# A three-layer block on one Trainium2 core: the first layer's columns from unscaled tiles, its head norms in two groups, its heads and pooling interleaved with columns

## The reference, cut to what matters

```python
h = rms_norm(x, norm_mix[0])
z = h @ w_in                                   # 1024 x 2048
u, q, k, v = jnp.split(z, [512, 1024, 1536], axis=-1)
p = multiscale_pool_minus_identity(u)          # windows 2, 4, 8, 16, one per 128 columns
p = einsum('bsgc,gcd->bsgd', p, pool_w) * pool_scale
a = moba_attention(q, k, v, q_gain, k_gain)    # 8 heads of 64
x = x + concatenate([p, a]) @ w_out

# inside moba_attention, with one block of 256 keys:
qn = q * rsqrt(mean(q * q) + eps) * q_gain     # per head and row; kn the same way
logits = qn @ kn.T * 64 ** -0.5 - slope[head] * distance, causal
out = softmax(logits) @ v
```

## Time and profile before

| what | value |
|---|---|
| median of 3 runs | 1214.41 us |
| the profiled execution's own time | 1214.9 us |
| its span in the profile | 1213.1 us |
| granted TensorE clock, mean | 0.96 of full speed |
| busy: PE / DVE / ACT / POOL | 1109.4 / 869.8 / 646.0 / 44.1 us |
| first matmul | 14.01 us |
| first long run of `pa_w_out` matmuls | 138.16 us |
| mean DMA rate | 165 GB/s |

### The profile page before, as it was taken

One profiled execution on the slowest core, in us unless ns is written; L12 is line 12 of the kernel. 1 busy time (PEld: TensorE's weight loads), 2 busy tenths in 40 slices (PEclk: granted clock), 3 DMA queues, 4 the chain that ended last, 5 costly groups with the idle time before them and its releaser, 6 DMA issues.

```text
span 1213.1 us, 20990 instructions
## 1 busy us (share of the span) xinstructions
PE 1109.4 (91%) x8548; PEld 1050.2 (87%) x8548; DVE 869.8 (72%) x1494; ACT 646.0 (53%) x1109; POOL 44.1 (4%) x50
## 2 busy tenths in 40 slices
PE   4769799999998988899999989899999989999996
PEld 3756499999997868789999988789989979999996
DVE  5666599888788448787877776998884577655543
ACT  6334467666554595566556568312224447876431
POOL 0000010000000200100000000000000002000010
PEclk9879899999998988899999989999999989999999
DMA  8422756655555556356666554122332354656541
GB/s 288 123 70 88 242 184 191 194 181 161 191 166 202 206 200 222 96 185 241 243 237 223 175 175 144 44 88 87 104 136 105 122 200 156 192 177 204 177 156 36
DMA packets 60576, 200.41 MB, mean 165 GB/s; under 512 B 6720, under 2 KB 12480, under 8 KB 60352
## 3 DMA queue, kind: packets, MB, share of 16 engines
q1 hardware_dynamic: 59040, 194.85, 48.7%
q10 hardware_dynamic: 1440, 4.22, 1.0%
HBM read 197.99 MB, written 1.05 MB: 164 GB/s over the span
## 4 chain that ended last, share of the span: by engine, by line
PE 71%; DVE 17%; ACT 8%; DMA 2%; issue 2%; SPq 0%; ACTq 0%; DVEq 0%
PE ps L451 71%; DVE wlo L1527 4%; ACT whi L1003 2%; ACT L1003 1%; DVE rst L1556 1%; DVE rq L1736 1%; DVE raw L1533 1%; DMA ring<-rg_w_in 1%; DVE raw L1527 1%; DVE hl L1527 1%; DVE xr L1533 1%; DMA ring<-pa_w_in 1%; ACT rr L1003 0%; ACT L L1003 0%; ACT raw L1003 0%
## 5 line engine op out<-in xcount | busy, mean ns | idle before, releaser
L451 PE MATMUL ps<-hh,whi 128*128 128x256 f32 (+1 forms) x1656 | 489.8, 296 | 56.2 <-DVE wlo L1527 42.7
L451 PE MATMUL ps<-hh,wlo 128*128 128x256 f32 (+1 forms) x1656 | 478.5, 289 | 0.0
L451 PE MATMUL ps<-hl,whi 128*128 128x256 f32 (+1 forms) x1656 | 476.7, 288 | 0.0
L1527 DVE TENSOR_TENSOR wlo<-ring,whi 128x1024 fp32r<-128x1024 f32 (+1 forms) x313 | 375.5, 1214 | 71.9 <-ACT whi L1003 71.0
L451 PEld LDWEIGHTS ps<-hh,whi 128*128 128x128 f32 x1656 | 324.2, 196 | 76.8 <-issue 31.5
L1003 ACT ACTIVATE whi<-ring 128x1024 fp32r<-128x1024 f32 (+1 forms) x313 | 322.6, 1039 | 96.7 <-PE ps L451 63.6
L451 PEld LDWEIGHTS ps<-hl,whi 128*128 128x128 f32 x1656 | 325.3, 196 | 1.5 <-issue 1.0
L451 PEld LDWEIGHTS ps<-hh,wlo 128*128 128x128 f32 x1656 | 324.4, 196 | 0.0
L451 PE MATMUL ps<-hidh,whi 128*128 128x256 f32 x608 | 172.3, 283 | 1.6 <-DVE wlo L1527 1.6
L451 PE MATMUL ps<-hidh,wlo 128*128 128x256 f32 x608 | 172.1, 283 | 0.0
L451 PE MATMUL ps<-hidl,whi 128*128 128x256 f32 x608 | 172.1, 283 | 0.0
(11 more groups left out here) (345 smaller groups left out, 1378.3 us busy)
## 6 DMA issues: line engine op xcount, KB each, us to landing
ring<-ffn_w_in SPq DMA_DIRECT2D x88, 512.0 KB, 4.2
ring<-ffn_w SPq DMA_DIRECT2D x64, 512.0 KB, 4.2
ring<-w_in SPq DMA_DIRECT2D x51, 512.0 KB, 3.6
ring<-ada_w SPq DMA_DIRECT2D x48, 512.0 KB, 4.9
ring<-ffn_w_out SPq DMA_DIRECT2D x32, 448.0 KB, 4.3
ring<-rg_w_in SPq DMA_DIRECT2D x20, 512.0 KB, 4.5
ring<-pa_w_in SPq DMA_DIRECT2D x16, 512.0 KB, 5.9
ring<-ffn_w_out SPq DMA_DIRECT2D x16, 512.0 KB, 3.6
```

The lines of the kernel that those rows point to most:

```text
L451: return e.matmul(o, l, r, start=start, stop=stop)
L1527: return e.tensor_tensor(o, a, b, op)
```

## The change

- All 16 columns of `pa_w_in` are taken from the tiles without the row's scale; `h_tiles(0)`, `early(0)` and the three `lift` go. u is multiplied by `rst` as it leaves PSUM, v by `tk` (the same scale with rows in partitions) as its transposition leaves PSUM, and for q and k the scale cancels in the head norm, where epsilon is multiplied by the row's mean square (`tk[:, 2]`).
- The head norms are done in two groups of four columns, with rows in partitions (`sums`): 8 matmuls with 2 output columns each give a 128x16 tile of means, so the root and the reciprocal work on 16 elements. For q the result is a scalar per partition in `scores`. For k ACT spreads it over 128x256 (`ivk`), PE turns it (`spread`), and DVE multiplies the column by it.
- `scores` starts from slope times distance, made ahead on POOL (`dms`, eight of 128x384, in space of `cosT` and `sinT`), and takes two instructions instead of one.
- One list, `ATTN`, sets the order on PE, ACT and DVE: a number is a column, N is `sums`, B `spread`, S `scores`, P the end of the softmax, T `turn_p`, V the transposition of v, O `values_of` (now two heads at once), G `pool_out`, A `mod_step`. Columns are in the order 4, 8, 5, 9, 6, 10, 7, 11, 12 to 15, 3, 2, 1, 0.
- The pooling's running sums move from DVE to POOL (`pooled`). `pah` and `pal` are made straight from PSUM. `L`, `PT` and `sm` have eight buffers.
- At the start the 32 vectors that the gains need are a DMA of their own, on ACT's queue, x comes in two DMAs instead of eight, and a dummy root loads ACT's table early. The sigmoid moves behind the first head norm.

```diff
+ATTN = [
+    4, 8, 5, 9, 6, ("N", 0), 10, ("B", 0), 7, ("S", 0), 11, ("S", 1), ("P", 0), 12, ("N", 1), ("S", 2), ("P", 1), ("T", 0),
+    13, ("B", 1), ("S", 3), ("P", 2), ("T", 1), ("A",), 14, ("S", 4), ("P", 3), ("T", 2), 15, ("S", 5), ("P", 4), ("T", 3), ("A",),
+    3, ("V",), ("S", 6), ("P", 5), ("T", 4), 2, ("O", 0), ("S", 7), ("P", 6), ("T", 5), ("A",), 1, ("O", 1), ("P", 7), ("T", 6),
+    ("A",), 0, ("T", 7), ("O", 2), ("G", 3), ("A",), ("G", 2), ("A",), ("O", 3), ("G", 1), ("A",), ("G", 0),
+]
...
-                early(0)
-                for i in range(3):
-                    give(("pa_w_in", 4 + i), at_dve, ("lift", i))
-                for ms in ([7, 8], [9], [10], [11], [12], [13], [14], [15]):
-                    project("pa_w_in", ms, 0)
-                    for i in HEAD_NORMS[ms[-1]]:
-                        head_norm(i)
...
+                    linear("pa_w_in", [c], pair(hh[:, :, 0:T], hl[:, :, 0:T]), 8, lambda k: hlow.wait_ge(e, (0, k)))
+                    if c < 4:
+                        give(("pa_w_in", c), at_dve, ("u", c))
+                    elif c < 12:
+                        give(("pa_w_in", c), at_act, ("qk", c - 4))
+                    else:
+                        give(("pa_w_in", c), at_act, ("v", c - 12))
+                    if c == 8:
+                        row_stats()
...
+                    mm(p[:, 0:T], ones, sqa[:, :], True, False)
+                    mm(p[:, 0:T], ones, sqt[:, 2, :], False)
+                    for z in range(2):
+                        zs = slice(z * 128, z * 128 + 128)
+                        mm(p[:, T + 2 * z:T + 2 * z + 2], sqa[:, zs], ones[:, 0:2], True, False)
+                        t = mm(p[:, T + 2 * z:T + 2 * z + 2], sqt[:, 2, zs], ones[:, 0:2], False)
+                    t.then_inc(*stat.up(0))
+                    give(("stat", 0), at_dve, "var")
...
+                def sums(g):
+                    p = take(("n", g))
+                    for j in range(2):
+                        for c in (4, 8):
+                            c += 2 * g + j
+                            a = qk_tile(c)[2]
+                            at_act.wait_ge(e, ("sq", c))
+                            for z in range(2):
+                                t = mm(p[:, z * 8 + 2 * a:z * 8 + 2 * a + 2], sq[:, a, z * 128:z * 128 + 128], blk[:, 0:128:64])
+                    t.then_inc(*at_pe.up(("n", g)))
+                    give(("n", g), at_dve, ("hm", g))
...
+                def spread(g):
+                    p = take(("b", g))
+                    at_act.wait_ge(e, ("ivk", g))
+                    for j in range(2):
+                        for z in range(2):
+                            t = mm(p[:, j * T + z * 128:j * T + z * 128 + 128], ivk[:, z, j, :], ident)
+                    t.then_inc(*at_pe.up(("b", g)))
+                    give(("b", g), at_dve, ("k", 2 * g + 1))
...
+                def column(c):
+                    feed(tail("pa_w_in", c))
+                    if 3 < c < 12:
+                        g, a = qk_tile(c)[1:]
+                        if g:
+                            at_pe.wait_ge(e, ("n", 0))
+                        act(sq[:, a, :], out_of("pa_w_in", c), ACT.Square).then_inc(*at_act.up(("sq", c)))
+                        at_dve.wait_ge(e, "gq")
+                        act(qk[:, c - 4, :], out_of("pa_w_in", c), ACT.Copy, gq[:, :] if c < 8 else P("k_gain")).then_inc(*at_act.up(("qk", c - 4)))
+                    elif c > 11:
+                        act(vf[:, c - 12, :], out_of("pa_w_in", c), ACT.Copy).then_inc(*at_act.up(("v", c - 12)))
+                    if c == 8:
+                        stats(0)
+                        at_dve.wait_ge(e, "var")
+                        act(tk[:, 1, :], tk[:, 0, :], ACT.Sqrt).then_inc(*at_act.up("root"))
...
+                def sums(g):
+                    at_dve.wait_ge(e, ("hm", g))
+                    act(iv[:, g, :], iv[:, g, :], ACT.Sqrt).then_inc(*at_act.up(("hr", g)))
+                    if g == 0:
+                        act(cpar[15], P("c", 0, 8), ACT.Sigmoid).then_inc(*ada_act.up("sig"))
+
+                def spread(g):
+                    at_dve.wait_ge(e, ("iv", g))
+                    if g:
+                        at_pe.wait_ge(e, ("b", 0))
+                    for z in range(2):
+                        i = iv[:, g, z * 8:z * 8 + 8].rearrange("p (j s) -> p j s", j=2)[:, :, 2:4].unsqueeze(3).to_broadcast([128, 2, 2, 64])
+                        t = act(ivk[:, z, :, :].rearrange("p j (s d) -> p j s d", s=2), i, ACT.Copy)
+                    t.then_inc(*at_act.up(("ivk", g)))
...
+                    act(pah[:, g, :], ps[where["po", g]][:, 0:T], ACT.Copy, P("pool_scale", g)).then_inc(*at_act.up(("pah", g)))
...
+                    act(pah[:, 4 + j, :], ps[where["o", j]][:, 0:T], ACT.Copy).then_inc(*at_act.up(("pah", 4 + j)))
...
+            e.dma_start(vec[:, 0:32], d["vec"][:, 0:32]).then_inc(*gains_in.up("all", 16))
             e.dma_start(cst[:, 0:384], d["cst"][:, 0:384]).then_inc(*ones_in.up("all", 16))
-            vecs_in.wait_ge(e, "all")
+            e.dma_start(vec[:, 32:], d["vec"][:, 32:]).then_inc(*vecs_in.up("all", 16))
+            at_dve.wait_ge(e, "dummy")
+            act(dmy[:, :], dmy[:, :], ACT.Sqrt).then_inc(*at_act.up("dummy"))
+            gains_in.wait_ge(e, "all")
             for m in range(8):
-                xin[m].wait_ge(e, m)
+                xin[m // 4].wait_ge(e, m // 4)
                 high_of_h(0, m)
-            feed(-4)
+                if m == 3:
+                    feed(-4)
...
-                    r = rq[:, i % 2, :]
-                    at_pe.wait_ge(e, ("hn", i))
-                    if i > 1:
-                        at_dve.wait_ge(e, ("qk", i - 2))
-                    ts(r, ps[where["hn", i]][:, 0:T], 1.0 / 64, 1e-6, MUL, ADD).then_inc(*at_dve.up(("hm", i)))
-                    at_act.wait_ge(e, ("hr", i))
-                    e.reciprocal(r, r).then_inc(*at_dve.up(("hi", i)))
...
-                    stt(qk[:, i, :], p, gq[:, :] if i < 4 else P("k_gain"), r, MUL, MUL).then_inc(*at_dve.up(("qk", i)))
...
+                def column(c):
+                    feed(tail("pa_w_in", c))
+                    if c < 4:
+                        mean.wait_ge(e, ("rst", 0))
+                        tt(u[:, c, 16:], out_of("pa_w_in", c), rst[:, :], MUL).then_inc(*at_dve.up(("u", c)))
...
+                def sums(g):
+                    at_pe.wait_ge(e, ("n", g))
+                    at_dve.wait_ge(e, "eps")
+                    for z in range(2):
+                        t = ts(iv[:, g, z * 8:z * 8 + 8], ps[where["n", g]][:, z * 8:z * 8 + 8], 1.0 / 64, tk[:, 2, 2 * z:2 * z + 1], MUL, ADD)
+                    t.then_inc(*at_dve.up(("hm", g)))
+                    at_act.wait_ge(e, ("hr", g))
+                    e.reciprocal(iv[:, g, :], iv[:, g, :]).then_inc(*at_dve.up(("iv", g)))
...
+                def spread(g):
+                    at_pe.wait_ge(e, ("b", g))
+                    for v in range(2):
+                        j = 2 * g + v
+                        at_act.wait_ge(e, ("qk", 4 + j))
+                        tt(qk[:, 4 + j, :], ps[where["b", g]][:, v * T:v * T + T], qk[:, 4 + j, :], MUL).then_inc(*at_dve.up(("k", j)))
...
+                    at_pool.wait_ge(e, ("dm", hd))
+                    at_dve.wait_ge(e, ("iv", g))
+                    at_pe.wait_ge(e, ("s", hd))
+                    stt(L[:, hd, 0:128], p[:, 0:128], iv[:, g, a:a + 1], dms[hd][:, 0:128], MUL, ADD)
+                    stt(L[:, hd, 128:384], p[:, 128:384], iv[:, g, 8 + a:9 + a], dms[hd][:, 128:384], MUL, ADD).then_inc(*at_dve.up(("L", hd)))
...
+            def pooled(g):
+                cur = u[:, g, :]
+                at_dve.wait_ge(e, ("u", g))
+                for w in range(g + 1):
+                    s = 1 << w
+                    nxt = (ta, tb)[w % 2]
+                    at_pool.wait_ge(e)
+                    e.tensor_tensor(nxt[:, 16:], cur[:, 16:], cur[:, 16 - s:16 + T - s], ADD).then_inc(*at_pool.up(("sum", g, w)))
+                    cur = nxt
+                at_pool.wait_ge(e)
+                e.tensor_tensor(cur[:, 16:], cur[:, 16:], cst2[:, 384 + g * T:384 + (g + 1) * T], MUL).then_inc(*at_pool.up(("mean", g)))
+                at_pool.wait_ge(e)
+                at_pe.wait_ge(e, ("vt", 1))
+                e.tensor_tensor(vf[:, g, :], cur[:, 16:], u[:, g, 16:], SUB).then_inc(*at_pool.up(("pool", g)))
+
+            e.memset(u[:, :, 0:16], 0.0)
+            e.memset(ta[:, 0:16], 0.0)
+            e.memset(tb[:, 0:16], 0.0).then_inc(*at_pool.up("zeros"))
+            pool_in.wait_ge(e, "all")
+            for hd in range(8):
+                e.tensor_scalar(dms[hd], cst2[:, 0:384], 2.0 ** -(hd + 1), None, MUL).then_inc(*at_pool.up(("dm", hd)))
+            for g in (3, 2, 1, 0):
+                pooled(g)
```

301 lines of the change are left out of this document (111 added, 190 removed).

## The result

The changed kernel takes **1177.4 us** (median of 4 runs, 1174.46 to 1179.18), the kernel before, on the same chip, 1214.93 (4 runs, 1213.67 to 1216.33): a ratio of 0.9688, 95% interval 0.9662 to 0.9715. The forecast was 1186.5 with a range from 1176 to 1199: faster as predicted, and by 9.1 us more.

The account below looks back on a forecast made before the run. PE was taken as the bound, losing time to standstills and half clock in the first layer. Terms 10.5 + 45.9 + 31.2 + 5 + 8.5, then 9.2, gave 110.3, 27.9 us less: 1187.0 profiled, median 1186.5, range 1176 to 1199.

Parts of the forecast that it names:

- the mark: Start of the first layer's product with `pa_w_out` on PE; forecast at 110.3 against 138.2, 27.9 us less.
- same work: Behind the first layer's `pa_w_out` start, both versions do the same work, so no further time was counted.
- first matmul: At the start, PE's first matmul at 10.5, 3.5 us earlier; bounds 9 and 13.
- half clock before the mark: PE at 1.2 GHz at the start and after each of two `ivk` waits, 8.5 us; bounds 2.8 and 20.
- waits for `ivk`: At both spreads PE waits 2.5 us for ACT's `ivk`; bounds none and 5 us, each.
- sums, two: PE's head-norm sums, 8 products with 2 output columns each; 2.2 us, twice; bounds 0.3 and 4.1.
- slot freed by the last-but-two modulation step, to the mark: Stage end: landing and splitting of `pa_w_out`'s first chunk, 9.2 us, with PE standing for 4.
- Waits that don't bite: Rival at the spreads: `ivk` is ready, 5 us of waits and 5.6 of half clock go; 1176, chance 0.16.
- DVE late through POOL: Rival in the first layer: POOL holds up DVE's splits and second-group norms, 11 us more; 1197, chance 0.23.
- The gain is given back: Rival behind the first stage: freeing ring slots sets the rate, next chunks no earlier; 1200 to 1212, chance 0.06.
- slower: Rival in the first stage: short waits keep PE at half clock, 68 us more if throughout; 1255, chance 0.02.
- A wait of 4 us before `pa_w_out`: Sign at the stage's end: PE stands 4 us before `pa_w_out`, whose matmuls start at about 110.

Follow-up runs that it names:

- the short reciprocal: Kernel before, its eight head-norm reciprocals working on 16 of 256 elements, output not the reference's; 1202.44 us, ratio 0.9907.
- the old start: Changed kernel with eight DMAs for x, one vector DMA ahead, first weight split after all pieces, no dummy root; 1177.59 us, ratio 0.9704.
- the steps moved: Changed kernel with three modulation steps moved from the first mixer's end into the first feed-forward part; 1169.04 us, ratio 0.9631.
- the old order: Changed kernel with `ATTN` in the kernel before's sequence: all q, k, v columns first, then heads with pooling between; 1173.17 us, ratio 0.9673.
- the two experiments: Kernel before with reciprocals on 16 elements, 1202.44 us; changed kernel with four 128x256 reciprocals before each group's small one, 1187.48 us.
- the eight that nobody waited for: Changed kernel with four 128x256 reciprocals on scratch data behind each head-norm group's small reciprocal, eight in all; 1187.86 us, one run.
- the late sigmoid: Changed kernel with the sigmoid, and with it a table load, moved behind the first spread; 1176.05 us, ratio 0.9693.
- both kernels with moved steps: Changed kernel with three modulation steps moved to the feed-forward part, 1169.04 us; the same plus the sigmoid behind the first spread, 1168.72 us.

## Why the prediction was right, and where it was wrong

**The accounting.** The forecast for the profiled execution was 1187.0 with the mark at 110.3; the mark came at 100.4, 9.9 earlier, and the execution took 1179.18, 7.8 less. So the whole miss lies in the stage that I summed up. From the mark on the prediction's "same work" held: the 2.1 us that came back are within the few microseconds by which executions differ. Term by term:

| term | forecast | measured |
|---|---|---|
| first matmul | 10.5 | 11.09 |
| half clock before the mark | 8.5 | 3.7 |
| waits for `ivk` | 5.0 | 2.76 |
| sums, two | 4.4 | 3.5 |
| spreads, two | 2.4 | 1.8 |
| slot freed by the last-but-two modulation step, to the mark | 9.2 | 8.8 |
| rest of PE's own work, by difference | 70.3 | 68.7 |

(Together they make 110.3 and 100.4. A sum takes 49.19 - 47.42 = 1.77, a spread 36.69 - 35.78 = 0.91, and in the rest scores take 0.85 for 0.9 and transpositions 0.3 to 0.48 for 0.5. The slot was freed at 91.59, when the step had ended, and not half-way through it, so my sum lacked half a step, 0.5.)

**The step that failed most: half clock.** I wrote that PE would run "again after each of the two waits, as from 31.57 to 37.50" at 1.2 GHz, 2.8 us each time. Of the three times only the first was there, and it cost 2.0 (21 matmuls 0.213 apart, until about 15.6, each 0.094 longer than at full clock). The waits of 1.68 and 1.08 us cost none. In their place came a stretch of 1.7 us (4 x 0.40, and 0.1 before it) that I had not foreseen, at the second sums, with no wait ahead of it.

My rule, half clock after each wait, was drawn from one row with 2.71 us. The traces together show that it holds for the long ones (2.71, 4.13, 5.00, 6.84), though not always from the first matmul on. The kernel before had this row, which I didn't read:

```profile
53.18 0.39 PE L451 MATMUL ps<-hh,whi 128*128 128x256 f32 x1 [2.99 <-DVE rq L1530]
```

Twelve matmuls behind it start 0.12 apart, and only from 54.7 on are they 0.21 apart. Among the shorter ones the length does not decide: 1.08, 1.13, 1.45, 1.68 and the 2.01 at 54.67 of the short reciprocal were followed by full clock, its 1.85 at 60.11 and the 1.85 of the old start by half. The kernel before had, on PE's timeline,

```profile
116.02 1.13 PE L451 MATMUL ps<-vf,pw 128*128 128x256 f32 x2 [2.22 <-DVE vf L1527]
...
125.75 0.55 PE L611 MATMUL ps<-cst,L 128*128 128x128 f32 x3 [1.69 <-DVE L L1530]
```

both followed by a granted clock of 0.54 to 0.61, where PE was doing scores, transpositions and products with values, not columns. But columns are no safeguard: with the steps moved, a wait of 1.54 at 122.42, three matmuls behind one of 0.36, was followed by half clock in the middle of a column. And the program alone doesn't decide either: the same kernel waited 2.53 us for `mrow` at 111.38 in its first trace, with half clock behind it, and 2.52 at 112.15 in its second, at full clock. What exactly decides stays open. What the rows do tell is that a price of 2.8 us for each short wait was too high: two such waits cost nothing here, and a third stretch came where there was no wait.

**The waits.** The mechanism was right at both places, ACT's queue ahead of `ivk`, and the size was twice too large. At the first I added the pieces of ACT's work up as if they began with the sums; the bound is the moment when PE finishes column 10, and what ACT does behind it. Removing 1.5 us ahead of that moment changed the wait by 0.23. At the second, PE's own half-clock stretch gave ACT more time: it stood still for 0.89 us in front of `vf`, the column that PE had just finished, and the wait is `vf` and two `ivk`. In the same order at full clock, with the old start, the wait is 1.85, nearer to my 2.5, and in the old order 1.18. (Of my 6.7 us for ACT the pieces make 6.1; the other 0.6 stood for its wait for DVE, and that one measured 0.60.)

**The rivals.** *Waits that don't bite*, 1176, is the nearest in time, but not quite what happened: half of its 5 us of waits stayed, the half clock behind them went, and a stretch of 1.7 came elsewhere. The result lies only 1.4 us inside the lower end of my range, which was this rival's time; that the range held is in part luck. *DVE late through POOL* did not happen: PE waited for no split and no logits before it came to `pa_w_out`. One row looks like the lock: POOL's `vf` took 1.79 us at 76.52 beside a weight split that DVE began at the same moment, against 0.74 to 0.86 for its like. The rule of the Trainium skill (SBUF — State Buffer, section "SBUF: two separate sides"), that one of the two holds the shared port for its whole instruction and the other waits, fits that row, but here it was POOL that was held up: the split took 1.21. The splits before the mark took 1.251 us on average for 1.221, 0.5 us in all for 18, and with the pooling back on DVE 1.265, so the pooling on POOL isn't what lengthened them. Moving the pooling back to DVE changed nothing at the fourth addition. *The gain is given back* and *slower* found no support in the changed kernel: the fourth addition is 38.3 us earlier and the median 37.5 lower, and the clock from 10 to 100 us was 0.98.

**What paid.** By the fourth addition the change is worth 38.3 us. The start is 6.5 of it (2.9 at the first matmul by the two traces, 3.5 by the experiment, the rest is half clock and 0.8 of waiting), though the medians with and without it lie only 2.3 apart. Short reciprocals are 14 to 17 in the traces of the two experiments, and 12 by the median of the first; a good part of it is DVE's time and not the chain, since the eight that nobody waited for cost 12.1. The order is nothing or slightly worse. The pooling on POOL is nothing now; in the old kernel its instructions on DVE stood for 4.4. The remaining 10 to 20 belong to what I didn't try apart: the columns without the scale, with no hole at 31.57, and the other DVE instructions of head norms and logits. The parts were tried in different kernels and need not add up exactly.

**The end.** "A wait of 4 us before `pa_w_out`" was right (4.13), and the step behind it, that the slot freed by a modulation step sets it, was shown by moving the steps.

## What to carry to other kernels

A wait has to be worked out from the last thing that can't be moved in front of it, not from the sum of what its engine does: ACT's shorter queue gave nothing, while eight reciprocals that nobody needed cost 12 us because two in-order queues stood behind them. Shrink what one engine does in a serial chain (a reciprocal of 16 elements for one of 256) before you reorder around it; here the order, the largest part of the edit, paid nothing. And look at what frees the slot of the next stage's first weight: moving three cheap steps out of its way was worth 6 to 8 us.

## What the runs showed of the chip

- Half clock came without a standstill: PE ran from 36 on without a gap, then 16 records of matmuls with 2 output columns (1.77 us), four of a score and three of a transposition, and from 50.2 to 53.1 the granted clock was near 0.50. With the sums between columns (the old order) the clock stayed at 1.00 there, and with the old start too, in the changed order. The same kernel again, the late sigmoid, the pooling on DVE and both kernels with moved steps had the stretch.
- One kernel in two executions: a wait of PE of 2.53 us with half clock behind it (0.50 from 112 to 114), and the same wait, 2.52 us, with none. The half clock at the start, too, ended between 14.1 and 17.1 us in kernels that are the same up to there, which moves all that follows by up to 0.7 us.
- A product of 128x128 by 2 output columns costs 0.22 us (two records of 0.11), where one with 256 output columns costs 0.12 at full clock in rounded form and 0.51 in plain float32.
- POOL does an addition of 128x256 in 0.61 us at its shortest (0.73 in other rows), and multiplies 128x384 by a constant in 1.34 (eight in 10.8 us). DVE's reciprocal of 256 elements takes 1.76, of 16 elements 0.25.
- ACT's table loads take 1.28 us each; taking one out of the first spread's way shortened the wait by 0.23.
- The same later stages took 831 to 839 us in different executions, so a microsecond gained early is seen at a mark close behind it and not in a single total.
